# A per-partition scalar operand in GpSimd's softmax normalisation

## The reference, cut to what matters

```python
def one_block(qblk):
    sc = jnp.einsum('bqhgd,bkhd->bhgqk', qblk, k).astype(jnp.float32) * scale
    p = jax.nn.softmax(sc, axis=-1).astype(v.dtype)
    return jnp.einsum('bhgqk,bkhd->bqhgd', p, v)
```

## Time and profile before

| | value |
|---|---|
| median of three runs | 2954.46 us |
| the profiled execution | 2955.78 us, its span 2954.0 us |
| TensorE (PE) | 96% busy, mean granted clock 0.977 |
| VectorE (DVE) | 55% busy |
| ScalarE (ACT) | 39% busy |
| GpSimd (POOL) | 26% busy |
| line 952 on GpSimd | 128 instructions, 140.8 us, 1104 ns mean |

### The profile page before, as it was taken

The page is one execution under the profiler, slowest core; times in us unless marked ns, Lnnn a source line. Parts: engine busy times, 40 slices in busy tenths (PEclk is TensorE's granted clock), DMA queues, the critical chain, the costliest instruction groups (busy, mean ns, idle before and its releaser), DMA issues.

```text
span 2954.0 us, 33945 instructions
## 1 busy us (share of the span) xinstructions
PE 2821.5 (96%) x12934; PEld 2314.5 (78%) x12934; DVE 1617.6 (55%) x2079; ACT 1161.6 (39%) x1792; POOL 754.4 (26%) x621
## 2 busy tenths in 40 slices
PE   8898999999988989999999888999999999999998
PEld 6676887888866768878888776888887789888887
DVE  5787446334267874464542796565523558565532
ACT  5576234222245762342222464333222338532222
POOL 2464113313124641133131262022200003122210
PEclk9999999999999999999999898999999989999999
DMA  3011222323220112223232211223232210122332
GB/s 137 29 43 36 93 98 81 101 93 100 95 77 29 43 36 93 97 82 107 93 100 95 77 36 58 97 94 100 94 107 93 85 57 1 57 93 94 99 100 100
DMA packets 76274, 236.42 MB, mean 80 GB/s; under 512 B 9904, under 2 KB 19904, under 8 KB 76128
## 3 DMA queue, kind: packets, MB, share of 16 engines
q1 hardware_dynamic: 74928, 231.05, 23.7%
q0 software_dynamic: 928, 3.27, 0.3%
q10 hardware_dynamic: 272, 0.06, 0.0%
HBM read 228.31 MB, written 2.10 MB: 78 GB/s over the span
## 4 chain that ended last, share of the span: by engine, by line
PE 85%; DVE 8%; ACT 3%; issue 2%; DMA 1%; POOL 1%; SPq 0%; POOLq 0%; DVEq 0%; ACTq 0%
PE bank L1941 27%; PE bank L1943 27%; PE bank L1942 27%; PE bank L2281 2%; PE bank L2108 1%; DVE S5S L1788 1%; DMA RAWW<-weights 1%; DVE STAT L1616 1%; DVE WL L1505 1%; ACT WH L1163 1%; DVE S5S L1779 1%; DVE PHL L1510 0%; PE bank L2050 0%; DVE CF L1566 0%; PE bank L2188 0%
## 5 line engine op out<-in xcount | busy, mean ns | idle before, releaser
L1505 DVE TENSOR_TENSOR WL<-RAWW,WH 128x1024 fp32r<-128x1024 f32 (+2 forms) x424 | 573.4, 1356 | 771.9 <-ACT WH L1163 771.7
L1941 PE MATMUL bank<-UH,WH 128*128 128x512 f32 (+1 forms) x1920 | 762.0, 397 | 45.7 <-DVE UL L1515 29.4
L1942 PE MATMUL bank<-UL,WH 128*128 128x512 f32 (+1 forms) x1920 | 754.2, 393 | 0.0
L1943 PE MATMUL bank<-UH,WL 128*128 128x512 f32 (+1 forms) x1920 | 754.2, 393 | 0.0
L1163 ACT ACTIVATE WH<-RAWW 128x1024 fp32r<-128x1024 f32 (+2 forms) x424 | 431.2, 1027 | 384.2 <-DMA RAWW<-weights 383.6
L1941 PEld LDWEIGHTS bank<-UH,WH 128*128 128x128 f32 (+1 forms) x1920 | 364.5, 190 | 133.0 <-issue 49.0
L1942 PEld LDWEIGHTS bank<-UL,WH 128*128 128x128 f32 (+1 forms) x1920 | 365.0, 190 | 78.4 <-issue 2.7
L1943 PEld LDWEIGHTS bank<-UH,WL 128*128 128x128 f32 (+1 forms) x1920 | 364.2, 190 | 77.8
L1941 PE MATMUL bank<-HH,WH 128*128 128x512 f32 x512 | 199.2, 389 | 0.0
L1942 PE MATMUL bank<-HL,WH 128*128 128x512 f32 x512 | 199.2, 389 | 0.0
L1943 PE MATMUL bank<-HH,WL 128*128 128x512 f32 x512 | 199.2, 389 | 0.0
(11 more groups left out here) (358 smaller groups left out, 4737.2 us busy)
## 6 DMA issues: line engine op xcount, KB each, us to landing
RAWW<-weights SPq DMA_DIRECT2D x424, 512.0 KB, 3.4
X<-x SPq DMA_DIRECT2D x8, 256.0 KB, 5.5
FF<-tables POOLq DMA_DIRECT2D x2, 1024.0 KB, 7.4
U<-S5U SPq DMA_DIRECT2D x32, 64.0 KB, 2.0
out<-FF SPq DMA_DIRECT2D x16, 128.0 KB, 1.8
GEL<-U SPq DMA_DIRECT2D x112, 16.0 KB, 1.8
S5B<-s_b POOLq DMA_DIRECT2D x1, 512.0 KB, 4.5
S5C<-s_c POOLq DMA_DIRECT2D x1, 512.0 KB, 3.7
```

The lines of the kernel that those rows point to most:

```text
L1505: dve.tensor_tensor(slot_words(WL, c % SLOTS, size), slot_words(RAWW, c % SLOTS, size), f32(slot_words(WH, c % SLOTS, size)), ALU.subtract ...
L1941: nc.tensor.matmul(out_, w[0], x_[0], start=start, stop=False, **how)
L1942: nc.tensor.matmul(out_, w[0], x_[1], start=False, stop=False, **how)
L1943: return nc.tensor.matmul(out_, w[1], x_[0], start=False, stop=stop, **how)
```

## The change

The second input of the multiplication was a 128x1 tile stretched to 128x512 with a step of zero, read as a tensor. It becomes the scalar operand of a `tensor_scalar`, one number per partition, read from the same place. Inputs, output, waits, signals and the place in the queue are the same.

```diff
                 elif st.kind == "att_normalise":
                     pool.wait_ge(recip.sem, recip.after(l, st.u))
-                    pool.tensor_tensor(TMP[:, st.u % 4, :], TMP[:, st.u % 4, :],
-                                       STAT[:, 2, st.u % 4:st.u % 4 + 1].to_broadcast([P, SEQ]), ALU.mult
+                    pool.tensor_scalar(TMP[:, st.u % 4, :], TMP[:, st.u % 4, :], STAT[:, 2, st.u % 4:st.u % 4 + 1], None, ALU.mult
                                        ).then_inc(normed.sem, 1)
```

## The result

The changed kernel takes 2974.32 us (median of 4 runs, 2972.5 to 2976.22), the kernel before 2954.57 us on the same chip (4 runs, 2954.16 to 2957.22). The ratio is 1.0063, with a 95% interval from 1.0049 to 1.0078: slower by 19.8 us. The forecast was 2946.8 us; the time lies inside the range and on the other side of no change. The profiled execution took 2972.5 us, with a span of 2970.7.

A forecast was written before the change was run, and what follows sets the result against it. TensorE was taken to set the pace (busy 96% of the span, GpSimd 26%). Terms 3.2 + 0.33 + 0.2 + 0.1 gave 3.8 us per layer, 7.7 in both, hence 2946.8 us; range 2942 to 3006 us.

The forecast's parts named there:

- D: Length of one changed L952 multiplication on GpSimd, 512 elements: bounded at 0.71 and 1.9 us, taken as 0.71 against 1.04.
- The one-operation row: Profile row of one-operation tensor_scalar, 0.293 us for 32 elements: extra as fixed cost gives 0.71 us, per element 1.9 us.
- First hole: TensorE's 3.88 us idle in each layer's GQA, behind CF: claimed to fall to 1.1 us, 3.2 us gained per layer.
- an open train: Gap in GpSimd's unbroken row of instructions at the first hole just when CF arrives, so CF takes 0.73 us.
- Above that the train stays closed, and the gain is what L952 loses: At the first hole, with D above 0.83 us, GpSimd's row has no gap and the gain is a few tenths.
- the limit of 0.83 us: Largest D at which the second L952 ends by 126.05, leaving GpSimd a gap at the first hole.
- Second hole: TensorE's 2.79 us idle in each layer's GQA: CF still waits for GpSimd's row to end at 141.47; gain 0.33 us.
- the third hole: TensorE's 2.14 us idle in each layer: L938 also needs the sine product, so it stays near 2.1; gain 0.1 us.
- Everywhere else TensorE's work hides it: Outside the counted places, L952 ends well before its transposes and TensorE's work hides it: gain nothing.
- the operand costs per element: Rival, chance 0.33: D is 1.9 us, GpSimd nearly closed in MLA, 23 to 39 us slower in both layers, 2992 us.
- The rival's 0.8 us a head: In MLA, VectorE's share of a head goes from 10.6 to 13.1 us, over the head's 12.3; 6.4 us a layer.
- Its threshold, D of 1.35 us: D from which that rival decides: six L952 cost 1.9 us a layer, with low clock near 6 us in all.

The follow-up runs named there:

- two operations: Kernel before with line 952 as a two-operation tensor_scalar, times r and then times 1.0, in all 128 units: 2943.51 us, ratio 0.9954.
- Four quarters: Kernel before with the broadcast tensor_tensor of line 952 cut into four of 128 columns in all 128 units: 2981.08 us, ratio 1.0088.
- GQA alone: Kernel before with the one-operation scalar form only in the 32 GQA units of each layer, broadcast tensor in MLA: 2955.93 us, ratio 1.0002.

## Why the prediction was wrong

**The step that failed** is the first term: D, put at 0.71 us and measured at 1.56. The one-operation row had two readings, and I took the one in which its extra 0.08 us is fixed. It is cost per element (2.5 ns). The small row was the only one of this kind of instruction in the trace, and I weighed against it that the memset and the two-operation form run at one stream's rate. Neither is the same instruction.

**First hole: the mechanism stands for a short D.** With D at 0.69 us (two operations) it came as written: CF at 0.74 us, the hole at 1.09, the clock at 1.00 in both stretches. After the change, CF is short too, but in another way than by an open train:

```profile
128.16 1.28 POOL L931 TENSOR_TENSOR FF<-FF 96x512 f32<-96x512 f32 x1
129.22 0.78 DVE L1565 SCALAR_TENSOR_TENSOR CF<-CF,LP,RCQ 128x512 f32<-128x512 f32 x1
129.43 1.99 POOL L952 TENSOR_SCALAR TMP<-TMP,STAT 128x512 f32<-128x512 f32 x1
...
131.48 0.66 PE L2107 MATMUL bank<-MAT,TMP 128*128 128x128 f32 x4 [1.20 <-POOL TMP L952]
132.10:136.20 4.10, 2.91 (x12) 1.72 (x11) 4.10 (x5) 2.24 (x5) 4.10 (x3) 1.00 0.00 0
```

The train is closed (L952 starts 1.27 us after L931), CF begins ahead of L952 and ends beside it, 0.56 us after L931 does, and L952 stretches to 1.99 us. The hole is 1.20 us and the clock behind it 1.00. The transposes now wait for L952 itself. "Above that the train stays closed, and the gain is what L952 loses" was therefore wrong: the limit of 0.83 us assumed that every form shuts VectorE out alike. Four quarters, as long but of the old form, have CF at 4.94 us in the same place.

**Second hole.** Forecast 0.33 us less, since CF would still wait for the end of the train. With two operations it doesn't: the train is closed (L938 from 134.22, L953 from 135.49, L949 from 136.59), and CF, from 135.25, takes 0.81 us. TensorE's largest idle time behind the smaller latent is 0.67 us (before 2.79), and the fall of the clock behind it is gone, which the sum had left out. The two holes are 4.9 us shorter together, and TensorE's idle time in GQA fell by 3.4, so 1.5 us came back in smaller waits (the forecast gave back 1.26). That and both falls of the clock make the 6.1 us of GQA, in place of a forecast of 3.5 for the two holes. After the change the hole is 1.45 us, waiting for L952. The clock falls behind it in layer 1, and in layer 2, behind a hole of 1.43 us, it doesn't (last row):

```profile
144.14 0.66 PE L2107 MATMUL bank<-MAT,TMP 128*128 128x128 f32 x4 [1.45 <-POOL TMP L952]
144.00:148.00 4.00, 3.44 (x11) 2.66 (x12) 3.55 (x6) 2.89 (x8) 4.00 (x4) 0.66 0.00 0
...
967.27:971.27 4.00, 2.96 (x13) 2.03 (x13) 3.57 (x7) 2.90 (x8) 4.00 (x4) 1.00 0.00 0
```

**MLA and the third hole.** I wrote that the third hole stays near 2.1 us, since L938 waits for the sine product anyway. With two operations it is 2.15 us, as written. But that holds only while the queue ahead of L938 isn't longer than the way to that product. The before rows show L938 starting 0.14 us behind it: there is no room for a longer instruction. After, L938 starts at the end of the queue and the hole is 3.08 us:

```profile
265.03 0.80 PE L1940 MATMUL bank<-MKH,MQH 96*128 96x512 f32 x1 [3.08 <-DVE MQL L1509]
```

I had looked only at what a shorter instruction gives there, a tenth of a us, and the two sides are not symmetric. "Everywhere else TensorE's work hides it" is true of a shorter L952, too; it is false of a longer one, by 1.33 us a head.

**The rival "the operand costs per element"** had the right kind and the right side: D 1.9 against 1.56, 2992 us against 2974. It came near for a reason that is only half its own, so part of it is luck. It saw VectorE shut out 0.83 us longer at each instruction, the trains of GQA worse, and up to 1 us a head of low clock. The clock in the MLA heads stays at 1.00, and the trains of GQA got better in both layers. VectorE does wait longer in MLA, at RL (before, then after, min/median/max):

```profile
L1510 DVE TENSOR_TENSOR RL<-FF,RH x26: 671/693/1756, 67.9 to 1059.7; 96x512 fp32r<-96x512 f32 x18, 128x512 fp32r<-128x512 f32 x8
```

```profile
L1509 DVE TENSOR_TENSOR RL<-FF,RH x26: 671/2250/2694, 71.0 to 1079.5; 96x512 fp32r<-96x512 f32 x18, 128x512 fp32r<-128x512 f32 x8
```

But RL waits beside L931 and L942, which are `tensor_tensor`. In the head shown, RL starts 2.47 us after the reciprocal of u3 (before 2.57), L942 3.04 us after it (before 2.50). RL then meets the end of L931 and the whole of L942 (start us, us; the L942 after):

```profile
215.60 2.39 DVE L1509 TENSOR_TENSOR RL<-FF,RH 96x512 fp32r<-96x512 f32 x1
216.17 1.27 POOL L942 TENSOR_TENSOR MKL<-KVF,MKH 64x512 fp32r<-64x512 f32 x1
```

The rival's 0.8 us a head stood for VectorE's total; the 1.33 us measured are mainly GpSimd's queue. Its threshold, D of 1.35 us, was not tested.

**Small slips in the working.** 129.48 - 126.7 is 2.78 us and not 2.75, and 1.9 - 1.04 is 0.86 and not 0.83. TensorE has a hole of 2.31 us in each layer that the prediction doesn't name; it waits for UL behind the attention and is the same in every kernel. None of this moves the forecast.

**The rule on the shared port.** The Trainium skill (SBUF — State Buffer, Who interferes with whom) has the two engines exclude each other for a whole instruction when VectorE has two SBUF inputs and GpSimd reads SBUF. The broadcast `tensor_tensor` agrees roughly (3.98 us for three instructions that take 1.88 with one input in PSUM). The one-operation scalar form doesn't: 1.97 us beside instructions of 1.55 us each, the first of which had begun 0.47 us before VectorE's three. The prediction's "by that rule the old and the new form hold the port alike" was wrong by that measurement, and the measurement decides.

## What to carry to other kernels

Price an instruction by the exact form that will run (one operation or two, pointer or tensor), and where the trace has only a small one of it, measure a large one before building on either reading: here 1.0 as a second operation turned a loss of 20 us into a gain of 12.6. Compare the same place in both layers before naming a cause: behind the second hole of the changed kernel the clock fell in one layer and not in the other. Ask what an edit does in both directions at each place: work that hides a shorter instruction needs not hide a longer one, and the slack to look for is that of the next instruction in the same queue, not of whoever reads the output. An engine that is busy for a quarter of the kernel can set the pace for a stage if its instructions stand in a row between two others' work.

## What the runs showed of the hardware

- GpSimd's one-operation `tensor_scalar` on f32 costs 2.5 ns an element (1.55 us for 512 with a pointer, 1.46 with an immediate). With a second operation it is 0.67 us, a copy about 0.6, the broadcast `tensor_tensor` 1.04. Why one operation is slower than two stays open.
- How far GpSimd keeps VectorE out depends on the form: three VectorE instructions with two SBUF inputs took 1.97 us beside the one-operation form, 2.38 beside two operations, 2.71 beside a copy, 3.98 beside a broadcast `tensor_tensor`, 4.65 beside one of two tensors (for `scalar_tensor_tensor` 2.51, 2.94, 3.22, 3.98 and 4.64). This was measured once, at 512 elements of f32 alone, and one CF of 2.95 us (GQA alone, layer 2) doesn't fit it.
- The length of a hole of TensorE and how busy it was ahead of it don't tell whether the clock falls. In the changed kernel a hole of 1.45 us in layer 1 had a granted clock of 0.66 over the next 4 us (1.2 GHz for most of them), and its twin of 1.43 us in layer 2 had 1.00 (2.4 GHz). TensorE had been busy for 6.66 and 6.65 of the 8 us before them, at 1.00. In four quarters, MLA holes of 1.10 us (layer 1) and 1.09 us (layer 2), with TensorE busy for all of the 8 us before, had 0.68 and 1.00 behind them. What decides it no run shows.
